# Both recurrent gates of a head in one product, on half of the array's rows

## What is computed

```python
xc = conv(xb) + conv_b                                   # 4 taps, by channel
xg = xc.reshape(B, S, LRU_BLOCKS, W // LRU_BLOCKS)       # 8 blocks of 64
r = sigmoid(einsum('bsnc,ncd->bsnd', xg, w_a) + b_a)
i = sigmoid(einsum('bsnc,ncd->bsnd', xg, w_x) + b_x)
log_a = -LRU_C * r * softplus(-lam)
a = exp(log_a)
u = sqrt(-expm1(2.0 * log_a)) * i * xc
_, h = associative_scan(combine, (a, u), axis=1)         # h = a * h_before + u
return h * gelu(yb)
```

## Time and profile before

| | |
|---|---|
| median of three runs | 1106.75 us (1106.3 to 1108.09) |
| profiled execution, its time | 1105.81 us |
| its span, first to last instruction | 1103.9 us |
| PE busy | 1084.5 us, 98% |
| DVE busy | 570.9 us, 52% |
| ACT busy | 470.3 us, 43% |
| the gates' products (L712), both layers | 7.2 us busy, 32 passes |

### The profile page before, as it was taken

The page is one execution under the profiler, slowest core; times in us unless marked ns, Lnnn a source line. Parts: engine busy times, 40 slices in busy tenths (PEclk is TensorE's granted clock), DMA queues, the critical chain, the costliest instruction groups (busy, mean ns, idle before and its releaser), DMA issues.

```text
span 1103.9 us, 14485 instructions
## 1 busy us (share of the span) xinstructions
PE 1084.5 (98%) x5868; PEld 752.5 (68%) x5868; DVE 570.9 (52%) x911; ACT 470.3 (43%) x758; POOL 2.6 (0%) x5
## 2 busy tenths in 40 slices
PE   8999999999999999999999999999999999999998
PEld 6998888888886344434479988888888753434433
DVE  6669774656565123223277687745665542313222
ACT  6677666565543001001266857656655410010101
POOL 0000000000000000000000000000000000000000
PEclk9999999999999999999999999999999999999999
DMA  9545544253877999999974354452349789999996
GB/s 379 226 153 189 193 153 153 84 221 153 311 293 311 429 428 429 426 427 427 421 275 182 129 194 153 167 213 87 145 163 368 255 371 430 427 427 426 429 428 275
DMA packets 24243, 313.15 MB, mean 284 GB/s; under 512 B 3184, under 2 KB 3312, under 8 KB 5744
## 3 DMA queue, kind: packets, MB, share of 16 engines
q1 hardware_dynamic: 23904, 312.22, 70.2%
q10 hardware_dynamic: 272, 0.00, 0.0%
HBM read 311.16 MB, written 1.05 MB: 283 GB/s over the span
## 4 chain that ended last, share of the span: by engine, by line
PE 87%; DMA 6%; DVE 4%; ACT 2%; issue 1%; DVEq 0%; SPq 0%; ACTq 0%
PE slot L665 35%; PE M L1013 16%; PE slot L1045 9%; PE slot L648 8%; DMA arena<-in_w_up 6%; PE slot L890 3%; PE slot L955 2%; PE slot L594 2%; PE M L848 1%; PE M L826 1%; PE slot L968 1%; PE M L968 1%; PE M L797 1%; PE M L837 1%; PE M L712 1%
## 5 line engine op out<-in xcount | busy, mean ns | idle before, releaser
L1472 DVE TENSOR_TENSOR w_lo<-ring,w_hi 128x1024 fp32r<-128x1024 f32 x198 | 238.0, 1223 | 145.9 <-ACT w_hi L1106 144.3
L1106 ACT ACTIVATE w_hi<-ring 128x1024 fp32r<-128x1024 f32 x200 | 207.7, 1054 | 96.3 <-PE slot L665 67.8
L665 PE MATMUL slot<-w_hi,hT_hi 128*128 128x512 f32 x480 | 192.0, 400 | 0.0
L665 PE MATMUL slot<-w_lo,hT_hi 128*128 128x512 f32 x480 | 187.2, 390 | 0.0
L665 PE MATMUL slot<-w_hi,hT_lo 128*128 128x512 f32 x480 | 187.0, 389 | 0.0
L1908 DVE TENSOR_TENSOR arena<-arena,M 128x512 f32<-128x512 f32 x16 | 11.0, 688 | 201.5 <-PE M L1013 201.5
L665 PEld LDWEIGHTS slot<-w_lo,hT_hi 128*128 128x128 f32 x480 | 90.1, 188 | 19.3
L665 PEld LDWEIGHTS slot<-w_hi,hT_hi 128*128 128x128 f32 x480 | 90.2, 188 | 18.6 <-issue 0.8
L665 PEld LDWEIGHTS slot<-w_hi,hT_lo 128*128 128x128 f32 x480 | 90.3, 188 | 18.2 <-issue 0.5
L648 PE MATMUL slot<-hT_hi,w_hi 128*128 128x256 f32 x256 | 73.4, 287 | 0.0
L648 PE MATMUL slot<-hT_hi,w_lo 128*128 128x256 f32 x256 | 72.4, 283 | 0.0
(11 more groups left out here) (302 smaller groups left out, 1652.1 us busy)
## 6 DMA issues: line engine op xcount, KB each, us to landing
ring<-in_w_mix SPq DMA_DIRECT2D x48, 2048.0 KB, 7.8
ring<-in_w_down SPq DMA_DIRECT2D x18, 2048.0 KB, 19.5
arena<-in_w_gate SPq DMA_DIRECT2D x12, 2048.0 KB, 19.0
ring_down<-in_w_gate SPq DMA_DIRECT2D x12, 2048.0 KB, 20.1
ring<-in_w_up SPq DMA_DIRECT2D x10, 2048.0 KB, 19.8
ring_up<-in_w_up SPq DMA_DIRECT2D x6, 2048.0 KB, 16.5
ring_odd<-in_w_up SPq DMA_DIRECT2D x6, 2048.0 KB, 20.8
arena<-in_w_up SPq DMA_DIRECT2D x6, 2048.0 KB, 22.2
```

Of the source, the lines that this page charges most:

```text
L665: last = mm(o[:, t * 512:(t + 1) * 512], h[:, 2 * n + cc, t * P:(t + 1) * P], w[:, cc * 512:(cc + 1) * 512], start=n == cc == k == 0, stop ...
L1106: A(piece_of(w_hi, i), source(i), ACT.Copy).then_inc(hi_ready.sem, 1)
L1472: v.tensor_tensor(piece_of(w_lo, i), source(i), piece_of(w_hi, i), ALU.subtract)\
```

## The change

The two gates of one block now come from one product. The stored matrix of a chunk, `w_ax`, has the two blocks of `w_a` on its diagonal and the two of `w_x` off it. A product takes 64 rows of it (one block, `hh`) and all 128 columns: 64 of its output partitions are r and 64 are i of that block. The first block of each chunk goes to M0, the second to M1, in turn. i comes out on the other half of the partitions than its channels, so its sigmoid reads one half of the partitions and writes the other. There are sixteen sigmoids on 64 partitions instead of eight on 128; `gate_i` is done first, then a piece of weights, then `gate_r`. All sigmoids wait for all products, and one signal at the end stands for both gates. The room that `w_x` had in the parameter tile is now `probs`, which with `w_ax` is the scratch of the attention, as the two matrices were before; the tile keeps its size.

```diff
-                def lru_gates(name, dst):
-                    wv = q(name).rearrange("p (c n) -> p c n", c=WC)
+                def both_gates():
+
+                    pe.wait_ge(xc_ready.sem, xc_ready.at(l, 1))
+                    pe.wait_ge(z_abs.sem, z_abs.at(l, 1))
+                    wv = q("w_ax").rearrange("p (c n) -> p c n", c=WC)
                     for cc in range(WC):
-                        last = mm(dst[:, cc * T:(cc + 1) * T], wv[:, cc, :], xcv[:, cc, :], start=True, stop=True)
+                        for hh in range(2):
+                            rows = slice(hh * 64, (hh + 1) * 64)
+                            last = mm((M0, M1)[hh][:, cc * T:(cc + 1) * T], wv[rows, cc, :], xcv[rows, cc, :],
+                                      start=True, stop=True)
                     last.then_inc(lru_ps.sem, 1)
-
-                def both_gates():
-                    pe.wait_ge(xc_ready.sem, xc_ready.at(l, 1))
-                    lru_gates("w_a", M1)
-                    pe.wait_ge(z_abs.sem, z_abs.at(l, 1))
-                    lru_gates("w_x", M0)
...
                 act.wait_ge(lru_ps.sem, lru_ps.at(l, 1))
-                for cc in range(WC):
-                    w = A(gate_r[:, cc * T:(cc + 1) * T], M1[:, cc * T:(cc + 1) * T], ACT.Sigmoid,
-                          bias=q("b_a")[:, cc:cc + 1])
-                w.then_inc(lru_sig.sem, 1)
+
+                def lru_sigmoid(gate, bias, hh, rows):
+
+                    own = slice(hh * 64, (hh + 1) * 64)
+                    for cc in range(WC):
+                        cols = slice(cc * T, (cc + 1) * T)
+                        w = A(gate[own, cols], (M0, M1)[hh][rows, cols], ACT.Sigmoid, bias=q(bias)[own, cc:cc + 1])
+                    return w
+
+                lru_sigmoid(gate_i, "b_x", 0, slice(64, 128))
+                lru_sigmoid(gate_i, "b_x", 1, slice(0, 64))
                 split_ahead(J_OG, 2)
-                act.wait_ge(lru_ps.sem, lru_ps.at(l, 2))
-                for cc in range(WC):
-                    w = A(gate_i[:, cc * T:(cc + 1) * T], M0[:, cc * T:(cc + 1) * T], ACT.Sigmoid,
-                          bias=q("b_x")[:, cc:cc + 1])
-                w.then_inc(lru_sig.sem, 1)
+                lru_sigmoid(gate_r, "b_a", 0, slice(0, 64))
+                lru_sigmoid(gate_r, "b_a", 1, slice(64, 128)).then_inc(lru_sig.sem, 2)
...
-        def blocks(w):
+        def blocks(own, other):
             o = np.zeros((P, WC, P), np.float32)
             for n in range(2 * WC):
                 b = (n % 2) * 64
-                o[b:b + 64, n // 2, b:b + 64] = w[n]
+                o[b:b + 64, n // 2, b:b + 64] = own[n]
+                o[b:b + 64, n // 2, 64 - b:128 - b] = other[n]
             return o.reshape(P, -1)
...
-        put("w_a", blocks(a["lru_w_a"][l]))
-        put("w_x", blocks(a["lru_w_x"][l]))
+        put("w_ax", blocks(a["lru_w_a"][l], a["lru_w_x"][l]))
```

More of the change, by code:

```diff
@@ L142 @@
     ("gate_b", 2), ("out_gain", 1), ("conv_w", TAPS * WC), ("conv_b", WC), ("b_a", WC),
-    ("b_x", WC), ("lam", WC), ("w_a", WC * P), ("w_x", WC * P), ("q_gain", P), ("k_gain", P),
+    ("b_x", WC), ("lam", WC), ("w_ax", WC * P), ("probs", WC * P), ("q_gain", P), ("k_gain", P),
     ("low", DC * LOW), ("gate_up", 2 * P)])
@@ L261, in build @@
         prob = h0(1024, 1792)
-        wa0 = PAR["w_a"][0]
+        wa0 = PAR["w_ax"][0]
         probT = prm[:, wa0:wa0 + 768]
@@ L330, in build @@
         pad_ready, xc_ready = Signal("pad_ready", 1), Signal("xc_ready", 1)
-        lru_ps, lru_sig, lru_at = Signal("lru_ps", 2), Signal("lru_sig", 2), Signal("lru_at", 1)
+        lru_ps, lru_sig, lru_at = Signal("lru_ps", 1), Signal("lru_sig", 2), Signal("lru_at", 1)
         lru_m, lru_sqrt, brB_ready = Signal("lru_m", 1), Signal("lru_sqrt", 1), Signal("brB_ready", 1)
@@ L707, in _ @@
                 xcv = xc.rearrange("p (c t) -> p c t", c=WC)
-                def lru_gates(name, dst):
-                    wv = q(name).rearrange("p (c n) -> p c n", c=WC)
-                    for cc in range(WC):
-                        last = mm(dst[:, cc * T:(cc + 1) * T], wv[:, cc, :], xcv[:, cc, :], start=True, stop=True)
-                    last.then_inc(lru_ps.sem, 1)
                 def both_gates():
                     pe.wait_ge(xc_ready.sem, xc_ready.at(l, 1))
-                    lru_gates("w_a", M1)
                     pe.wait_ge(z_abs.sem, z_abs.at(l, 1))
-                    lru_gates("w_x", M0)
+                    wv = q("w_ax").rearrange("p (c n) -> p c n", c=WC)
[4 more added lines that the diff above has]
+                                      start=True, stop=True)
+                    last.then_inc(lru_ps.sem, 1)
                 channel_major(J_OG, hT_hi, hT_lo, middle=both_gates)
@@ L1194, in _ @@
                 act.wait_ge(lru_ps.sem, lru_ps.at(l, 1))
-                for cc in range(WC):
-                    w = A(gate_r[:, cc * T:(cc + 1) * T], M1[:, cc * T:(cc + 1) * T], ACT.Sigmoid,
-                          bias=q("b_a")[:, cc:cc + 1])
-                w.then_inc(lru_sig.sem, 1)
-                split_ahead(J_OG, 2)
-                act.wait_ge(lru_ps.sem, lru_ps.at(l, 2))
-                for cc in range(WC):
-                    w = A(gate_i[:, cc * T:(cc + 1) * T], M0[:, cc * T:(cc + 1) * T], ACT.Sigmoid,
-                          bias=q("b_x")[:, cc:cc + 1])
-                w.then_inc(lru_sig.sem, 1)
+                def lru_sigmoid(gate, bias, hh, rows):
+                    own = slice(hh * 64, (hh + 1) * 64)
+                    for cc in range(WC):
+                        cols = slice(cc * T, (cc + 1) * T)
[3 more added lines that the diff above has]
+                lru_sigmoid(gate_i, "b_x", 1, slice(0, 64))
+                split_ahead(J_OG, 2)
+                lru_sigmoid(gate_r, "b_a", 0, slice(0, 64))
+                lru_sigmoid(gate_r, "b_a", 1, slice(64, 128)).then_inc(lru_sig.sem, 2)
                 act.wait_ge(lru_sig.sem, lru_sig.at(l, 2))
```

## The result

| | before | after |
|---|---|---|
| median of four runs | 1107.35 us | 1115.32 us |
| lowest, highest | 1106.30, 1108.09 | 1114.43, 1116.36 |
| profiled execution, its span | 1105.81, 1103.9 | 1115.87, 1114.0 |

The medians are 8.0 us apart. The ratio, which is not the quotient of these two medians, is 1.0079 with a 95% interval of 1.0067 to 1.0091: the change makes the kernel slower by 0.8%. The forecast was slower by 0.4%, and the time lies 0.5 us above the top of its range. The forecast started from 1106.75, the median of three runs; a fourth run, 1107.94, is in the median here.

The account below looks back on a forecast made before the run. TensorE, 98% busy, was taken as the bound: sigmoids delay a weight piece by 3.06 us, swallowing the products' 1.54 us gain, so it starts 2.26 us later per layer; 1106.75 + 4.5 = 1111.3 us, range 1109.0 to 1114.8.

Parts of the forecast that it names:

- What bounds the kernel, and which piece is tightest: TensorE, busy 98%, bounds; the first query job's fourth weight piece is tightest, with margins of 0.84 and 0.83 us.
- The entry that the forecast asked for: Sign in TensorE's list of waits: a new entry, L665 for w_lo, of 3.8 us, twice; wrong if under 1.5.
- Products: Gate products on TensorE: sixteen half-height passes run as eight pairs, 1.91 us instead of 3.45, gaining 1.54 us per layer.
- Sigmoids: Gate sigmoids on ScalarE: eight more of 64x256 at 0.36 us each, 2.88 us more per layer.
- Q3: Fourth weight piece of the first query job; predicted to start 2.26 us later per layer, after TensorE waits 3.8 us.
- The sum without the clock: Late start of the first query job's fourth piece, 2.26 us per layer: 4.5 us for two layers, giving 1111.3.
- The clock: Rival: TensorE's clock falls in the wait at L665; one fall gives 1113.5, one in each layer 1115.7; chance 0.12.
- The price of a fall: Time lost by slow TensorE passes after a clock fall: 2.2 us, from 22 passes at the program's start.
- half-price sigmoids: Rival: half-height sigmoids on ScalarE cost half, 0.18 us each; 1105.5 us; chance 0.07.
- Halves that do not overlap: Rival: the halved products on TensorE do not pair, sigmoids start 1.81 us later; 1114.5 us; chance 0.08.
- The range: Whole kernel's forecast time: 1109.0 to 1114.8 us, up to the unpaired case and down for half of the unforeseen.

Follow-up runs that it names:

- the filled wait: Changed kernel with 14 idle products put on TensorE ahead of the fourth piece of the first query job: 1111.63 us, ratio 1.0047 against the kernel before.
- the sigmoids alone: Kernel before with full-height products, only its 8 sigmoids on 128 partitions cut into 16 on 64: 1113.39 us, ratio 1.0056 against the kernel before.

## Why the prediction was wrong, step by step

*What bounds the kernel, and which piece is tightest*: right. The entry that the forecast asked for, L665 waiting for w_lo twice, is the first of the list, with 3.67 and 3.64 us where 3.8 stood.

*Products*: right in mechanism. Pairs were shown at 256 columns, and the sixteen records take 1.92 us. The gain was put at 1.54 and is 1.3: the new group was right, but the old one was taken as sixteen passes of 0.216, 3.45 together, and the next line had begun after 3.26.

*Sigmoids*: 0.36 was right from one sigmoid to the next. What the sum left out are the changes from one half of the partitions to the other and to the 128-partition piece: three more of 0.12 us per layer ahead of the tanhs, so that the eight more sigmoids cost 3.25 us where 2.88 stood. With a start that came 0.11 later instead of 0.18, the exponentials and VectorE's step behind them came 3.35 us later, where 3.06 stood. By 0.3 us per layer that made Q3's start 2.57 later instead of 2.26. The page "ScalarE: Activation LUTs" of the Trainium skill, section "What ACT_TABLE_LOAD costs", gave an estimate of 0.40. The trace has 0.36 from one sigmoid to the next on 64 and on 128 partitions and does not agree; that the mean of 0.39 lies close to the estimate comes from the changes of half.

*The sum without the clock*: 4.5 us; the filled wait gives 5.2. The step was sound.

*The clock*: this is the step that failed. The sum that gave 1111.3 had nothing in it for slower passes behind the wait; the fall stood as a rival with 0.12, one fall in each layer at 1115.7 with 0.04. Both layers of the profiled execution fell, which cost 1.59 + 1.67 = 3.3 us; with the wait filled and no fall the kernel took 1111.6, close to the sum. The only row set beside the wait of 3.6 us was the end of the program, where the clock had stayed full for 3.5 us after TensorE's last pass; no reason is given for the 0.12 beyond that. The runs show that this row does not bear on how long a wait can be without a fall: waits of 2.4 us were followed by a fall in both layers of one execution, and of two waits of 2.8 in another execution one was and one was not. The moment of the fall is not tied to the wait's end either: it came between 0.4 us before TensorE started again and 1.2 us behind. What sets it within that span stays open here. The price of a fall was 2.2 us, taken from the program's start, and is 1.6 to 1.7. The rival's 1115.7 lies near the measured 1115.3 because a price too high by 1.1 us for two falls and a late piece too cheap by 0.6 partly cancel, which is luck. The page "TensorE: Matmul & The Clock Gate" of the Trainium skill, section "HAM oscillation", says that TensorE starts slow again after waits like these. The trace agrees with that in the second layer, and differs in the first, where the first 1.2 us after the wait still run at the full level.

*The rivals*: half-price sigmoids are refuted by the sigmoids alone (3.14 us for eight). Halves that do not overlap are refuted by the records in pairs, although their time, 1114.5, is only 0.8 off: the time alone could not have told it from the clock.

*The range* ended at 1114.8 because the two falls, with 0.04, were left out. The wait was as long as the one stretch without work behind which the trace had a fall, so a chance of one in two would have been the honest reading, and the range would have reached 1116.

## What to carry to other kernels

An engine that is 43% busy can still be on the path: look for the tightest hand-over to the busy engine behind the edit, and price the edit by its margin. Half the partitions did not make ScalarE's sigmoid cheaper here, and changing halves cost a little more, so work that is split by partitions belongs where nobody waits behind it, and the operands that the busy engine needs next go ahead of it in the queue. A new wait on TensorE as long as those here, 2.4 to 3.7 us, should be counted with the slow passes that may follow it, and can be filled with idle products until it is removed; products in a part of the wait, which left 2.8 us idle, did not hold the clock in every layer.

## What the runs showed of the hardware

Passes of 64 rows, from products in the two halves of the array's rows in turn, start in pairs, and a pair takes one pass's time: the sixteen passes take 1.92 us, where sixteen full-height ones of 256 columns of float32, 0.216 us apart, took 3.26. The turn into halves costs about 0.1 us (0.21 instead of 0.12 from the pass ahead).

A sigmoid of 256 columns on 64 partitions starts 0.36 us behind the one ahead, like one on 128, whether or not it writes another half than it reads; a change to the other half of the partitions, or from a half to an instruction on all of them, adds 0.12 us.

Behind waits of 2.4 to 3.7 us TensorE's granted clock fell to 0.50, its level of 1.2 GHz, in five of the six waits in the three profiles, and each of the two falls of the changed kernel lost 1.6 to 1.7 us. The fall came 1.2 us after the work had begun again in the first layer of the changed kernel, and 0.1 us before it in the second.
